# A pass over 16384 rows on one core: routing spread over more units, split activations in rows of 528 columns, rows of u loaded unit by unit

## What is computed

```python
q = (xb @ w_q).reshape(P_BLOCK, P_HEADS, 2, P_DKEY // 2)      # 8 heads, two halves of 128
s = jnp.einsum('thcd,hckd->thck', q, keys)                    # 128 scores for each half
s_top, i_top = lax.top_k(s, P_TOPK)                           # 16 of 128, twice
cand = s_top[:, :, 0, :, None] + s_top[:, :, 1, None, :]
best, pos = lax.top_k(cand.reshape(P_BLOCK, P_HEADS, P_TOPK * P_TOPK), P_TOPK)
gate = jax.nn.softmax(best, axis=-1)
u = jnp.take(u_tab, experts, axis=0)
act = jax.nn.gelu(jnp.einsum('thkd,td->thk', u, xb))
vv = jnp.take(v_tab, experts, axis=0)
return jnp.einsum('thk,thkd->td', gate * act, vv)
```

## Time and profile before

| | |
|---|---|
| median of three runs | 4600.81 us |
| profiled execution | 4607.75 us, its span 4606.0 us |
| PE busy | 4353.5 us (95%) |
| mean granted clock of PE | 0.970 |
| pass over u, layer 0 | from 887.03 us to 1708 us |
| pass over u, layer 1 | the same program; the page counts 6144 of its products in all |

### The profile page before, as it was taken

One profiled execution on the slowest core, in us unless ns is written; L12 is line 12 of the kernel. 1 busy time (PEld: TensorE's weight loads), 2 busy tenths in 40 slices (PEclk: granted clock), 3 DMA queues, 4 the chain that ended last, 5 costly groups with the idle time before them and its releaser, 6 DMA issues. The chain is left out here.

```text
span 4606.0 us, 66608 instructions
## 1 busy us (share of the span) xinstructions
PE 4353.5 (95%) x25931; PEld 3596.2 (78%) x25931; DVE 2889.4 (63%) x4715; ACT 1994.5 (43%) x4180; POOL 1368.4 (30%) x617
## 2 busy tenths in 40 slices
PE   8997898999999999999999977899999999999998
PEld 6964578877778878888879856887777887888887
DVE  3265745899655536666664368589965553666666
ACT  3221223278777832222232223327877773222222
POOL 0000001333433344444440000133343334444443
PEclk9997999999999999999999988999999999999999
DMA  4241224255866665555532330525686666455553
GB/s 165 82 140 43 84 68 103 74 149 167 246 196 176 186 209 187 194 203 181 201 125 86 113 107 24 116 63 150 178 251 187 179 178 212 183 201 194 185 197 121
DMA packets 553451, 703.26 MB, mean 153 GB/s; under 512 B 54361, under 2 KB 457426, under 8 KB 532658
## 3 DMA queue, kind: packets, MB, share of 16 engines
q1 hardware_dynamic: 545540, 681.40, 47.1%
q0 software_dynamic: 4608, 16.78, 1.2%
q10 hardware_dynamic: 2990, 0.82, 0.1%
HBM read 549.44 MB, written 145.01 MB: 151 GB/s over the span
## 5 line engine op out<-in xcount | busy, mean ns | idle before, releaser
L2937 PE MATMUL ps<-h_parts,u_parts 128*128 128x512 f32 x6144 | 1479.4, 397 | 13.0 <-PEq L2368 6.5
L2937 PEld LDWEIGHTS ps<-h_parts,u_parts 128*128 128x128 f32 x6144 | 1147.6, 189 | 276.9 <-POOL u_parts L2321 17.8
L3212 PE MATMUL ps<-w_parts,v_parts 128*128 128x512 f32 x4080 | 938.8, 389 | 0.0
L2321 POOL TENSOR_TENSOR u_parts<-u_turned,u_parts 128x1024 fp32r<-128x1024 f32 x256 | 618.9, 2418 | 990.8 <-ACT u_parts L2316 990.6
L3212 PEld LDWEIGHTS ps<-w_parts,v_parts 128*128 128x128 f32 x4080 | 765.8, 188 | 159.0
L2308 DVE STREAM_TRANSPOSE u_turned<-u_rows 128x1024 f32<-128x1024 f32 x256 | 317.6, 1241 | 298.2 <-POOL u_parts L2321 215.7
L3212 PE MATMUL ps<-first_w,first_v 128*128 128x512 f32 x2064 | 483.7, 390 | 7.3 <-PEq L2861 7.3
L3212 PEld LDWEIGHTS ps<-first_w,first_v 128*128 128x128 f32 x2064 | 388.4, 188 | 88.9 <-issue 8.1
L2846 ACT ACTIVATE onehots<-onehots,choice 128x128 fp32r<-128x128 f32 x1024 | 328.4, 399 | 8.7 <-DVE onehots L2819 8.7
L2850 ACT ACTIVATE onehots<-onehots,choice 128x128 fp32r<-128x128 f32 x1024 | 325.7, 393 | 0.0
L2316 ACT CAST u_parts<-u_turned 128x1024 fp32r<-128x1024 f32 x256 | 271.0, 1059 | 89.8 <-DVE u_turned L2308 89.8
(11 more groups left out here) (606 smaller groups left out, 5943.4 us busy)
## 6 DMA issues: line engine op xcount, KB each, us to landing
u_rows<-in_peer_u_dram SPq DMA_DIRECT2D x1024, 128.0 KB
u_rows<-in_peer_v_dram SPq DMA_DIRECT2D x86, 1024.0 KB, 4.9
hidden_tiles<-hidden SPq DMA_DIRECT2D x256, 256.0 KB
gate_matrices<-h SPq DMA_DIRECT2D x64, 1024.0 KB, 6.0
gates<-gate_matrices SPq DMA_DIRECT2D x32, 2048.0 KB, 7.9
u_turned<-hidden_tiles SPq DMA_DIRECT2D x256, 256.0 KB, 3.6
arena<-in_ada_w_dram SPq DMA_DIRECT2D x48, 1024.0 KB, 5.3
v_rows<-in_peer_v_dram SPq DMA_DIRECT2D x42, 1024.0 KB, 4.9
```

The costliest lines, as they stand in the source:

```text
L2321: s.nc.gpsimd.tensor_tensor(q.uTs[:, (n + 1) % 3, 1], q.uT[:, n % 2], q.uTs[:, (n + 1) % 3, 0].bitcast(F32), ALU.subtract).then_inc(q.u_re ...
L2937: ins = mm(ps[:, n % 2, :], q.uTs[:, (n + 1) % 3, wp, k, :], q.hs[:, xp, k, 0:T], start=k == 0 and (wp, xp) == (0, 0), stop=k == DT - 1 an ...
L3212: ins = nc.tensor.matmul(ps[:, o, :], q.vs[n % 3][:, vp, o * P:(o + 1) * P], q.ws[n % 3][:, wp], start=n == 0 and (vp, wp) == (0, 0), stop ...
```

## The change

- UNIT_WORK goes from 4.4 to 3.5: DVE takes fewer steps of routing in a unit. The planner then finds these units:

| | before | after |
|---|---|---|
| groups 0 to 3 routed in unit | 8, 17, 27, 37 | 10, 23, 37, 53 |
| first and last quad compared | 10, 115 | 12, 117 |
| samples' list made | 44 | 60 |
| first gather | 47 | 63 |
| dot products | 50 to 57 | 66 to 80, every second unit |
| sums of v's rows | 60 (four), 66 (four) | 83, 84, 85, 86, 89, 90, 91, 92 |
| load of the gates by SP | 118 | 120 |

- The samples' gathers, copies of activations and dot products come one by one, a step every second unit (SAMPLE_STEP = 2), and the sums one in a unit.
- `load_u` loads one unit with four DMAs of 128 KB. It is issued in SP's round n-6 for unit n, after unit n-4 has been transposed. Four semaphores stand for the four places (the buffer itself is the same size). Bytes and number of DMAs are the same.
- h_parts and the four tiles of `s.hh` get rows of NP = 528 floats (2112 bytes, 33 times 64; before 2080, 32.5 times 64). What is read and written of a row is the same. All these tiles start at a multiple of 64 bytes, before and after.

The diff, with repeated places left out:

```diff
--- before.py
+++ after.py
@@ -18,6 +18,7 @@
 N = T + B
+NP = 528
 HALF = (0, 256, N)
@@ -387,7 +388,7 @@
                 else:
-                    ins = nc.scalar.copy(hh[:, 0, k, :], h[:, k, :])
+                    ins = nc.scalar.copy(hh[:, 0, k, 0:N], h[:, k, :])
                 ins.then_inc(s.h_high.sem, 1)
@@ -2293,15 +2294,15 @@
 ADD_LAG = 3
-UNIT_WORK = 4.4
+UNIT_WORK = 3.5
+SAMPLE_STEP = 2
 WQ = 4
...
 
-    slot, pair = (n // TJ) % 2, n // TJ
-    if n % TJ == 0:
-        dve.wait_ge(q.u_loaded[slot].sem, q.u_loaded[slot].at(128 * (pair // 2 + 1)))
+    slot = (n // TJ) % 2
+    dve.wait_ge(q.u_loaded[n % 4].sem, q.u_loaded[n % 4].at(64 * (n // 4 + 1)))
     if n >= 2:
@@ -2322,13 +2323,10 @@
 
-def load_u(s, q, sp, layer, pair):
-    u_dram = s.io["peer_u"][layer].rearrange("(b p a j) (c f) -> a c p b j f", b=4, p=32, j=TJ, c=4)
-    slot = pair % 2
-    for j in range(TJ):
-        for c in range(4):
-            sp.dma_start(q.u[32 * c:32 * c + 32, slot, :, j, :], u_dram[pair, c][:, :, j]).then_inc(
-                q.u_loaded[slot].sem, 16)
+def load_u(s, q, sp, layer, n):
+    u_dram = s.io["peer_u"][layer].rearrange("(b p n) (c f) -> n c p b f", b=4, p=32, c=4)
+    for c in range(4):
+        sp.dma_start(q.u[32 * c:32 * c + 32, (n // TJ) % 2, :, n % TJ, :], u_dram[n, c]).then_inc(q.u_loaded[n % 4].sem, 16)
 
@@ -2384,7 +2382,8 @@
                 if k in (8, 10):
-                    load_u(s, q, sp, layer, (k - 8) // 2)
+                    load_u(s, q, sp, layer, k - 8)
+                    load_u(s, q, sp, layer, k - 7)
                 if k % 4 == 3:
@@ -2705,12 +2704,9 @@
             link(v.memset(r.hidm[:], 0.0))
-            while now[0] < unit["gather"] + 3:
-                yield 0.0
             for t in range(B):
-                if t == 4:
-                    while now[0] < dot_unit[3] + 4:
-                        yield 0.0
+                while now[0] < unit["gather"] + 3 + SAMPLE_STEP * t:
+                    yield 0.0
                 dve.wait_ge(q.us_loaded[t % 4].sem, q.us_loaded[t % 4].at(16 * (t // 4 + 1)))
@@ -2723,7 +2719,7 @@
             unit["sums"] = now[0]
-            while now[0] < unit["sums"] + 9:
+            while now[0] < unit["sums"] + 12:
                 yield 0.0
@@ -2894,7 +2890,7 @@
         for t in range(B):
-            sum_unit[t] = unit["sums"] - 1 if t < 4 else unit["sums"] + 5
+            sum_unit[t] = unit["sums"] - 1 + t if t < 4 else unit["sums"] + 1 + t
 
@@ -2904,7 +2900,7 @@
                 for t in range(B):
-                    if n == (unit["gather"] if t < 4 else dot_unit[t - 4] + 1):
+                    if n == (unit["gather"] + SAMPLE_STEP * t if t < 4 else dot_unit[t - 4] + 1):
                         if t < 4:
@@ -3020,10 +3016,10 @@
                         store_gates(group)
-                for pair in range(2, NK // TJ):
-                    if n == max(0, TJ * pair - 5):
-                        sp.wait_ge(q.turned.sem, q.turned.at(TJ * (pair - 1)))
-                        load_u(s, q, sp, layer, pair)
+                for unit_of in range(4, NK):
+                    if n == max(0, unit_of - 6):
+                        sp.wait_ge(q.turned.sem, q.turned.at(unit_of - 3))
+                        load_u(s, q, sp, layer, unit_of)
                 if n == exp_unit[0]:
@@ -3035,12 +3031,13 @@
                                  r.gate[:]).then_inc(q.s_stored.sem, 16)
-                    for t in range(4):
-                        sp.dma_start(xb_of[t], s.hrow_dram[t:t + 1, :].to_broadcast([P, D])).then_inc(q.xb_loaded[t].sem, 16)
                     sp.wait_ge(q.s_stored.sem, q.s_stored.at(32))
...
                         sp.dma_start(r.gateT[:], s.pgate_dram.rearrange("t p -> p t")).then_inc(q.s_turned.sem, 16)
+                for t in range(4):
+                    if n == unit["gather"] + SAMPLE_STEP * t - 2:
+                        sp.dma_start(xb_of[t], s.hrow_dram[t:t + 1, :].to_broadcast([P, D])).then_inc(q.xb_loaded[t].sem, 16)
                 for t in range(4, B):
@@ -3080,12 +3077,12 @@
     for i in range(4):
+        q.u_loaded[i].close(64 * NK // 4)
         q.xb_loaded[i].close(32)
...
         q.ss_stored[i].close(32)
-        q.u_loaded[i].close(128 * NK // TJ // 2)
         q.hid_stored[i].close(16 * NK // 2)
@@ -3247,7 +3244,7 @@
         with ExitStack() as own:
-            q.hs = s.sb(f"h_parts{layer}", [P, 2, DT, N], own, F32R)
+            q.hs = s.sb(f"h_parts{layer}", [P, 2, DT, NP], own, F32R)
             q.uTs = s.sb(f"u_parts{layer}", [P, 3, 2, DT, P], own, F32R)
@@ -3639,7 +3636,7 @@
     s.parts = s.bufs.take_parts(s, "odd_w_in_parts", 2, 2, DT, P)
-    s.hh = s.bufs.take_parts(s, "odd_h_parts", 2, DT, N)
+    s.hh = s.bufs.take_parts(s, "odd_h_parts", 2, DT, NP)
     s.proj = Projection(s, s.io["odd_w_in"][0], wide_blocks(0, 4096))
@@ -3996,7 +3993,7 @@
         q.sc_loaded = [Signal(s, f"sc_loaded{i}") for i in range(2)]
-        q.u_loaded = [Signal(s, f"u_loaded{i}") for i in range(2)]
+        q.u_loaded = [Signal(s, f"u_loaded{i}") for i in range(4)]
         q.hid_stored = [Signal(s, f"hid_stored{i}") for i in range(2)]
```

More of the change, by code:

```diff
@@ L3673, in odd_layer @@
     s.parts = s.bufs.take_parts(s, "odd_w_out_parts", 2, 2, DT, P)
-    s.hh = s.bufs.take_parts(s, "odd_y_parts", 2, DT, N)
+    s.hh = s.bufs.take_parts(s, "odd_y_parts", 2, DT, NP)
     s.modp = s.bufs.take([P, 2, DT, NB])
@@ L3793, in even_layer @@
 def even_layer(s, e):
-    s.hh = s.bufs.take_parts(s, "even_h_parts", 2, DT, N)
+    s.hh = s.bufs.take_parts(s, "even_h_parts", 2, DT, NP)
     mrows, e.rw = e.take([NB, 2, MU], [P, 4, N])
@@ L3833, in even_layer @@
     s.parts = s.bufs.take_parts(s, "even_w_out_parts", 2, 2, DT, P)
-    s.hh = s.bufs.take_parts(s, "even_y_parts", 2, DT, N)
+    s.hh = s.bufs.take_parts(s, "even_y_parts", 2, DT, NP)
     s.modp = s.bufs.take([P, 2, DT, NB])
```

## The result

| | before | changed |
|---|---|---|
| median of the runs, us | 4598.7 (4595.14 to 4601.54, 4 runs) | 4558.02 (4547.1 to 4560.46, 4 runs) |
| ratio, 95% interval | | 0.9907 (0.9889 to 0.9925) |
| profiled execution / its span, us | 4607.75 / 4606.0 | 4557.82 / 4556.1 |
| pass over u, layer 0 / 1, us | 821.0 / 821.8 | 796.2 / 797.3 |
| steady unit of 24 products, us | 5.588 | 5.568 |

The change makes the kernel about 41 us faster by the medians, 50 by the two profiled executions. The forecast was 94 us, more than twice as much; the time lies just inside the stated range (4484 to 4560 us). The pass over u accounts for all of the difference between the two profiled executions: 24.8 + 24.5 = 49.3 us.

The account below looks back on a forecast made before the run. PE, busy 95% of the span, was taken to bound the kernel, through its waits and its products' pace. Waits 52, padding 38 and 4 us off gave 4513.75 for the profiled execution, 4507 us by the median; range 4484 to 4560.

Parts of the forecast that it names:

- With 2112 bytes all rows begin on a block: Pass over u: rows beginning on 64-byte blocks bring products to the pass over v's pace; 38 us off, bounds 0 and 38.1.
- 4 elsewhere: Products of 256 and 264 columns in other passes: padding saves 0.8 ns each, 4 us; bounds 0 and 26.
- The bound of 6.2 ns a product: Pass over u: most that padding could save per product, 232.9 ns against 226.7 in the pass over v, over 6144 products.
- Rival 1: Padding gives nothing, since the pass over v's pace comes from rows a multiple of 2048 bytes apart; 4549 us, chance 0.26.
- The waits, 52 us: Pass over u: PE's waits shrink by 26.3 us a layer, 52 us for both; bounds 18 and 62.
- A: Units 0 to 11, paced by DVE: 13.3 of 15.3 us a layer go, 2 us stay at the third quad.
- B: Stretch from 1109 to 1173 us, DVE nearly full: 6 of 6.8 us a layer of idle PE and lower clock go.
- the small waits: Scattered waits of PE in the pass over u, some 2 us a layer: 1 us goes.
- C: Around 1221 us, a late load of u among gathers and copies: 6 of 7.4 us a layer go by loads and samples.
- what is late next: Next in line behind DVE was taken to be ACT, busy 79.6 of 100 us, becoming 82 at the shorter unit.
- ACT, the stores of hidden, and the full DMA engines: Samples fill the DMA engines for 70 us without delaying loads; a rival had hidden's stores lag and ACT wait, chance 0.08.
- Rival 3: The new row step is a worse one, products at 245.3 ns, slower than before: 4635 us, chance 0.04.

Follow-up runs that it names:

- p520: The changed kernel with rows of 520 floats again (2080 bytes apart), everything else as changed: 4566.11 us, ratio to before 0.9917.
- rows2304: The changed kernel with h_parts in rows of 576 floats (2304 bytes), mixers' rows back at 520, three small tiles moved: 4533.2 us, ratio 0.9846.
- steps_a: The changed kernel with rows of 520 floats, u's products reading overlapping rows 1792 (layer 0) or 1920 bytes (layer 1) apart; measuring only: 4547.19 us.
- best: As rows2304, with the picked list taken over three units after the pick in place of two: 4524.25 us, ratio 0.9822.
- only_loads: The kernel before with only u's rows loaded unit by unit with four signals: 4589.95 us, ratio 0.9972.
- only_work: The kernel before with only UNIT_WORK changed, 3.5 instead of 4.4: 4564.93 us, ratio 0.9908.
- settle3: As p520, with the picked list taken over three units after the pick in place of two: 4550.35 us, ratio 0.9879.
- steps_b: As steps_a, with a step of 2048 bytes in layer 0 and of none in layer 1: 4532.28 us.
- offsets: As steps_a with 1792-byte steps in both layers, first row 128 (layer 0) or 32 bytes (layer 1) later: units of 5.579 and 5.603 us.
- offsets2: As offsets, with every row 64 (layer 0) or 192 bytes (layer 1) behind a multiple of 256: units of 5.600 and 5.606 us.

## Why the prediction was right or wrong

**The failed step: "With 2112 bytes all rows begin on a block. ... nearest is the pass over v, so I take 38."** The term was 38 us in the pass over u and 4 elsewhere; it measured 9.4 (p520 against the changed kernel), and nothing elsewhere. The bound of 6.2 ns a product held: rows2304, with every row at the fast place, wins 5.1. Wrong was the block of 64 bytes. I saw two row steps with two prices and chose one of the many remainders by which 2048 and 2080 differ. The earlier trace rows can't tell between them, since the list holds 24 products in one line; the prediction says so, and took the full 38 us all the same. The starts of the single products in the trace of before wouldn't have settled it either. The even rows of a steady unit, which begin on a block of 64 bytes, stand at 232.4 ns there and the odd ones at 233.2, which looks like a case against the block; but by layer 1 of steps_a, where every second row is at the fast place and stands higher than its neighbours, such a mixture tells nothing. It took kernels with all rows at one place.

Rival 1 (4549 us, chance 0.26) came nearest, in its time (4558) and in its reason: the pass over v owes its pace to a larger multiple than 64, though not to 2048 but to 256. It had the padding at nothing for 9.4 us and the waits at 52 for 40, two misses that partly cancel.

The Trainium skill's page "SBUF — State Buffer" (section "Door 1: The DMA port swizzle (why `[64,N]` ≈ `[32,N]`)") gives cachelines of 16 bytes, and a penalty for each access that crosses to a new one. All row starts here lie on such a line, so by it the padding gives nothing. It gave 9.4 of the forecast 42 us, but the runs don't bear the rule out as the whole: rows on a 16-byte line cost 227.7 to 233.6 ns by their place in 256 bytes.

**The waits, 52 us: near in size, 40 measured** (p520's passes are 20.2 and 19.7 us shorter than before's). Point by point:

- A went as said: no wait in units 1 to 9, and with units of 5.56 us PE comes late enough for the third quads to find them ready. With the shorter units that the sum assumed, the remaining microseconds showed up in best, as written.
- B and the small waits went. C went too, but more than one part of the change cures it. The loads do what I gave them the 6 us for: in only_loads and in the changed kernel DVE's waits for rows of u are gone. DVE's lead does the same for PE by itself (only_work), which the forecast didn't see, so on top of the lead the loads and the samples add nothing that can be measured.
- What was missing is the answer to "what is late next" behind B and C. DVE ahead of PE now waits for PE at the takeover of the list; in before this was 12.3 us of DVE's time, in p520 37.2. Its price is settle3 against p520: 7.4 and 8.2 us in the two layers. Old waits that went: 27.6 and 27.9 us (settle3 against before), where I had 26.3. So the sum of the terms was right to 1.6 us a layer (the terms one by one weren't measured), and a new stall of 7 to 8 us a layer stood against it.
- ACT, the stores of hidden, and the full DMA engines (0.98 at 288 GB/s, forecast 289) cost nothing, as said. PE's idle time behind DVE's additions is 5.1 us a layer for "under 5".

Rival 3, a worse row step, didn't come: of the five places tried, none is more than 6 ns above the best.

Open is why the first five products of a unit stand at 228 to 236 ns even where all rows begin at 0 (later ones have 227), why mixtures cost a little more than their mean, and why their single rows don't show their own price. That an aligned row of 2048 bytes spans eight pieces of 256 bytes and any other nine would fit a price for a place off 0, but it isn't shown.

## What to carry to other kernels

Where two streams of products differ in pace and the cause is a guess about addresses, try one place for all rows at a time, since a mixture of places hides the price of each, even in the starts of its single instructions. Padding gives its full worth only if it brings every row to the fast place; here that took a step of nine times 256 bytes, not the next multiple of 64. And when an engine is given a lead, look at every instruction on it that waits for the engine it leads: these waits grow with the lead, and what is queued behind them comes late. Of several cures for one stall, count only one.

## What the runs showed of the hardware

TensorE's products of 512 float32r columns, at the full granted clock, follow each other at 227 ns when all moving rows begin at a multiple of 256 bytes in their partition (steps_a layer 0, steps_b, rows2304), and at 232 to 234 ns when all begin 32, 64, 128 or 192 bytes behind one (offsets, offsets2). The distance between rows, and whether they overlap, made no difference: steps of 0, 1792, 2048 and 2304 bytes give the same 5.47 us for 24 products.

For the mixers' products of 256 and 264 columns, steps of 2080 and 2112 bytes differ by 1 ns at most: medians of 118 and 121 to 122 ns from start to start in p520, 118 and 122 to 123 in the changed kernel. The queries' projection reads h_parts in the same pieces: with rows of 2304 bytes its products of 256 columns follow at 114 ns in place of 118 (p520), those of 264 at 121 in both.
